# Attention values with the value rows stationary and two heads side by side in the array

## The reference, cut to what matters

```python
# A: 4 heads, two softmax maps each (8 maps), output o1 - lam * o2
# B: 6 heads, latent attention          C: 6 heads, masked by distance
sc = einsum('bhqd,bhkd->bhqk', q, k) * scale
p  = softmax(sc, axis=-1)
o  = einsum('bhqk,bhkd->bhqd', p, v)      # 512 queries, 512 keys, width 64
```

## Time and profile before

| | |
|---|---|
| runs | 3307.59, 3308.88, 3309.75 us; median 3308.88 us |
| span of the profiled execution | 3305.6 us |
| PE, PEld busy | 3211.9 us, 2951.7 us (97%, 89%) |
| DVE, ACT, POOL busy | 2540.6, 1302.2, 1956.7 us (77%, 39%, 59%) |
| attention of layer 0, first matmul to last wait | 139.49 to 310.69 us |
| attention of layer 1, the same | 1782.31 to 1954.07 us |

### The profile page before, as it was taken

How to read it: one execution, slowest core, us unless ns; L and a number is a source line. 1 busy time by engine, 2 the same in 40 slices (tenths; PEclk the granted TensorE clock), 3 DMA queues, 4 the chain that set the end, 5 groups by cost and what they waited for, 6 DMA issues and landing times. The chain is left out here.

```text
span 3305.6 us, 64644 instructions
## 1 busy us (share of the span) xinstructions
PE 3211.9 (97%) x18498; PEld 2951.7 (89%) x18502; DVE 2540.6 (77%) x5451; ACT 1302.2 (39%) x2060; POOL 1956.7 (59%) x1556
## 2 busy tenths in 40 slices
PE   8999999999999999999999999999999999999997
PEld 8898889999999888888798988899999998888886
DVE  1466567888888899999924656588888888999998
ACT  2355234444444433333323542344444443333333
POOL 3445338888654466666544453488886544666665
PEclk9999999999999999999999999999999999999999
DMA  4001138999787799999820021399997877999996
GB/s 166 30 1 77 39 89 293 324 324 320 242 299 249 258 337 338 335 335 335 280 102 26 1 77 52 100 319 318 322 315 249 290 253 253 340 338 337 337 333 226
DMA packets 249399, 765.14 MB, mean 231 GB/s; under 512 B 28384, under 2 KB 95712, under 8 KB 241376
## 3 DMA queue, kind: packets, MB, share of 16 engines
q1 hardware_dynamic: 170400, 459.95, 42.1%
q0 software_dynamic: 73728, 268.47, 21.6%
q10 hardware_dynamic: 5184, 35.65, 3.0%
HBM read 677.98 MB, written 85.98 MB: 231 GB/s over the span
## 5 line engine op out<-in xcount | busy, mean ns | idle before, releaser
L687 POOL TENSOR_TENSOR st_lo<-st_raw,st_hi 128x1024 fp32r<-128x1024 f32 x290 | 697.8, 2406 | 463.9 <-ACT st_hi L949 454.3
L949 ACT CAST st_hi<-st_raw 128x1024 fp32r<-128x1024 f32 x544 | 569.9, 1048 | 663.0 <-PE ps L1993 632.8
L1902 PE MATMUL ps<-t_hi,st_hi 128*128 128x384 f32 (+1 forms) x2288 | 794.7, 347 | 0.0
L1903 PE MATMUL ps<-t_lo,st_hi 128*128 128x384 f32 (+1 forms) x2288 | 786.0, 344 | 0.0
L795 POOL TENSOR_TENSOR wt_lo<-w_f,wt_hi 128x384 fp32r<-128x384 f32 x256 | 418.1, 1633 | 319.5 <-ACT wt_hi L1080 319.4
L1906 PE MATMUL ps<-t_hi,st_lo 128*128 128x384 f32 (+1 forms) x2288 | 462.7, 344 | 0.0
L1902 PEld LDWEIGHTS ps<-t_hi,st_hi 128*128 128x128 f32 x2288 | 430.1, 188 | 10.5
L1903 PEld LDWEIGHTS ps<-t_lo,st_hi 128*128 128x128 f32 x2288 | 430.1, 188 | 9.8
L1906 PEld LDWEIGHTS ps<-t_hi,st_lo 128*128 128x128 f32 x2288 | 408.5, 188 | 11.0
L992 ACT ACTIVATE h_out<-ps 128x384 f32<-128x384 f32 x256 | 125.7, 491 | 696.7 <-PE ps L1906 592.7
L1993 PE MATMUL ps<-st_hi,wt_hi 128*128 128x512 f32 x1536 | 390.8, 390 | 2.7 <-ACT wt_hi L1080 2.7
(11 more groups left out here) (219 smaller groups left out, 5104.8 us busy)
## 6 DMA issues: line engine op xcount, KB each, us to landing
st_raw<-in_peer_u SPq DMA_DIRECT2D x256, 512.0 KB
st_raw<-in_peer_v SPq DMA_DIRECT2D x256, 512.0 KB
gelu_d<-h_out SPq DMA_DIRECT2D x256, 192.0 KB
h_in<-gelu_d SPq DMA_DIRECT2D x256, 192.0 KB
gates_d<-g_stage ACTq DMA_DIRECT2D x32, 1024.0 KB
g_ch<-gates_d SPq DMA_DIRECT2D x56, 512.0 KB, 6.1
w_raw<-in_w_in SPq DMA_DIRECT2D x16, 1168.0 KB, 5.3
st_raw<-in_peer_w_q SPq DMA_DIRECT2D x32, 512.0 KB
```

Source lines behind the costliest of these rows:

```text
L687: nc.gpsimd.tensor_tensor(st_lo[:, s].rearrange("p c f -> p (c f)"), st_raw[:, r], st_hi[:, s].rearrange("p c f -> p (c f)").bitcast(F32), ...
L949: nc.scalar.copy(st_hi[:, r % 2].rearrange("p c f -> p (c f)"), st_raw[:, r]).then_inc(st_h, 1)
L1902: nc.tensor.matmul(dst, st_hi[:, s, c], t_hi[:, c, rows], start=c == 0, stop=False)
L1903: nc.tensor.matmul(dst, st_hi[:, s, c], t_lo[:, c, rows], start=False, stop=False)
```

## The change

`values` changes its roles: the 128x64 block of values is stationary and the 128x128 block of turned probabilities streams. The two jobs of a pair are taken together: the even job's output goes to PSUM partitions 0 to 63, the odd job's to 64 to 127, of bank 6 (128 x 512: two heads' width x queries). `p_t` therefore holds both jobs of a pair; it moves, with a new tile `o_t`, into the space of `t_hi` and `t_lo`, which is idle during the attention. When a pair is there, ACT copies the bank to `o_t` (`keep_ot`), PE turns it back with four 128x128 transposes into bank 7 (`turn_back`), and one DVE operation of 128x512 per pair scales it into `o_all` (`finish`), where there was one of 128x256 per job.

The order on PE changes with it. The four calls of `values` for pair i stand in the odd job of pair i (block 0) and in the even job of pair i+1 (blocks 1, 2 and 3); `turn_back(i-1)` stands in the odd job behind `turn_qk`. The loops over pairs on PE and DVE are written out. Core of the diff:

```diff
-            def values(i, s, qb, kind):
-                j = 2 * i + s
-                if qb == 0:
-                    pe.wait_ge(o_ev, JOBS * l + j + 1)
-                pe.wait_ge((pt_dve, pt_act)[qb % 2], 2 * (JOBS * l + j) + qb // 2 + 1 + 1)
+            def values(i, qb):
+                if qb == 0:
+                    pe.wait_ge(ot_ev, PAIRS * l + i)
+                pe.wait_ge((pt_dve, pt_act)[qb % 2], 2 * (JOBS * l + 2 * i + 1) + qb // 2 + 1 + 1)
                 for k in range(TB):
-                    last = nc.tensor.matmul(ps[:, 6 + s, qb * VD:(qb + 1) * VD], p_t[:, qb, k], v, start=k == 0, stop=k == TB - 1)
+                    for s in range(2):
+                        last = nc.tensor.matmul(ps[s * VD:(s + 1) * VD, 6, qb * P:(qb + 1) * P], value_of(i, s, k),
+                                                p_t[:, s, qb, k], start=k == 0, stop=k == TB - 1)
...
+            def turn_back(i):
+                pe.wait_ge(ot_ev, PAIRS * l + i + 1)
+                pe.wait_ge(o_ev, PAIRS * l + i)
+                for tb in range(TB):
+                    last = nc.tensor.transpose(ps[:, 7, tb * P:(tb + 1) * P], o_t[:, tb * P:(tb + 1) * P], ident[:])
+                last.then_inc(ob_ps, 1)
...
+            def even(i):
+                j, kind = 2 * i, kinds[i]
+                score(j, 0, 2, kind)
+                turn_p(j, 0)
+                if i > 0:
+                    values(i - 1, 1)
+                turn_qk(j + 1, 1, kind)
+                score(j, 0, 3, kind)
+                turn_p(j, 1)
+                if i > 0:
+                    values(i - 1, 2)
+                score(j + 1, 1, 0, kind)
+                turn_p(j, 2)
+                if i > 0:
+                    values(i - 1, 3)
+                score(j + 1, 1, 1, kind)
+                turn_p(j, 3)
+
+            def odd(i):
...
+                score(j, 1, 2, kind)
+                turn_p(j, 0)
+                if ahead is not None:
+                    turn_qk(j + 1, 0, ahead)
+                if i > 0:
+                    turn_back(i - 1)
+                score(j, 1, 3, kind)
+                turn_p(j, 1)
+                if ahead is not None:
+                    score(j + 1, 0, 0, ahead)
+                turn_p(j, 2)
+                values(i, 0)
+                if ahead is not None:
+                    score(j + 1, 0, 1, ahead)
+                turn_p(j, 3)
...
+            for qb in range(1, TB):
+                values(PAIRS - 1, qb)
+            turn_back(PAIRS - 1)
# ACT
+            def keep_ot(i):
+                act.wait_ge(pv_done, PAIRS * l + i + 1)
+                nc.scalar.copy(o_t[:], ps[:, 6]).then_inc(ot_ev, 1)
...
                 if ahead is not None:
                     exponent(j + 1, 1 - s, 0)
+                if last_pair is not None:
+                    keep_ot(last_pair)
+                if ahead is not None:
                     exponent(j + 1, 1 - s, 1)
...
+            keep_ot(PAIRS - 1)
             act.wait_ge(sub_ss, l + 1)
# DVE
-                nc.vector.tensor_tensor(o_all[:, :, ds(j * VD, VD)],
-                                        ps[:, 6 + s, 0:TB * VD].rearrange("p (t d) -> p t d", t=TB),
-                                        row_inv[:, s].unsqueeze(2).to_broadcast([P, TB, VD]),
-                                        ALU.mult).then_inc(o_ev, 1)
+                nc.vector.tensor_tensor(o_all[:, :, ds(2 * i * VD, 2 * VD)].rearrange("p t (s d) -> p t s d", s=2),
+                                        ps[:, 7].rearrange("p (t s d) -> p t s d", t=TB, s=2),
+                                        row_inv[:, turn].rearrange("p s t -> p t s").unsqueeze(3).to_broadcast(
+                                            [P, TB, 2, VD]), ALU.mult).then_inc(o_ev, 1)
```

More of the change, by code:

```diff
@@ L164, in build @@
     assert T_D * 2 * GCH == 2 * DC * T
+    p_t = nc.alloc_sbuf_tensor_at("p_t", [P, 2, TB, TB, P], F32, offset=keep.end - 2 * DC * T * 4)
+    o_t = nc.alloc_sbuf_tensor_at("o_t", [P, T], F32, offset=keep.end - 2 * DC * T * 4 + 2 * TB * T * 4)
+    assert (2 * TB + 1) * T <= 2 * DC * T
     ident = keep.tile("ident", [P, P], F32)
@@ L1251, in job @@
                 if before:
-                    invert_sums(j - 1, 1 - s)
+                    invert_sums(j - 1, 1 - s, turn if s else 1 - turn)
                 if ahead is not None:
                     score(j + 1, 0, ahead)
-                if before:
-                    finish(j - 1, 1 - s)
-                keep_pt(j, 2)
+                if last_pair is not None:
+                    finish(last_pair, 1 - turn)
+                keep_pt(j, s, 2)
                 if ahead is not None:
@@ L1263, in _, with pair @@
             score(0, 1, "A")
[L1264 to L1273, removed]
+            def pair(i, turn, kind, after):
+                first_pair = isinstance(i, int) and i == 0
+                job(2 * i, 0, kind, kind, turn, before=not first_pair)
+                job(2 * i + 1, 1, kind, after, turn, None if first_pair else i - 1)
+            pair(0, 0, "A", "A")
+            pair(1, 1, "A", "A")
+            pair(2, 0, "A", "A")
+            pair(3, 1, "A", "B")
+            pair(4, 0, "B", "B")
+            pair(5, 1, "B", "B")
+            pair(6, 0, "B", "C")
+            pair(7, 1, "C", "C")
+            pair(8, 0, "C", "C")
+            pair(9, 1, "C", None)
             dve.wait_ge(sub_q, l + 1)
             nc.vector.tensor_reduce(sub_sq[:], o_q.rearrange("p t h d -> p (t h) d"), AX_X, ALU.add).then_inc(sub_ss, 1)
-            invert_sums(JOBS - 1, 1)
-            finish(JOBS - 1, 1)
+            invert_sums(JOBS - 1, 1, 1)
+            finish(PAIRS - 1, 1)
             at = at + JOBS
@@ L1825, in values @@
                 if qb == TB - 1:
                     last.then_inc(pv_done, 1)
[L1828 to L1833, removed]
-                turn_p(j, 0)
-                if before is not None:
-                    values(last_i, 1 - s, 2, before)
+            def turn_back(i):
[4 more added lines that the diff above has]
+                last.then_inc(ob_ps, 1)
@@ L1837, in job @@
+            def odd(i):
+                j, kind = 2 * i + 1, kinds[i]
+                ahead = kinds[i + 1] if i + 1 < PAIRS else None
+                score(j, 1, 2, kind)
+                turn_p(j, 0)
                 if ahead is not None:
-                    turn_qk(j + 1, 1 - s, ahead)
-                score(j, s, 3, kind)
+                    turn_qk(j + 1, 0, ahead)
+                if i > 0:
+                    turn_back(i - 1)
+                score(j, 1, 3, kind)
                 turn_p(j, 1)
-                if before is not None:
-                    values(last_i, 1 - s, 3, before)
@@ L1854, in _ @@
             score(0, 0, 1, "A")
-            job(0, 0, "A", "A")
-            job(0, 1, "A", "A", "A")
-            before, first = "A", 1
-            for kind, after, end in (("A", "B", JA // 2), ("B", "C", (JA + JB) // 2), ("C", None, JOBS // 2)):
-                if before != kind:
-                    job(first, 0, kind, kind, before)
-                    job(first, 1, kind, kind, kind)
-                    first += 1
-                with pe.Fori(first, end - 1) as i:
-                    job(i, 0, kind, kind, kind)
-                    job(i, 1, kind, kind, kind)
-                job(end - 1, 0, kind, kind, kind)
-                job(end - 1, 1, kind, after, kind)
-                before, first = kind, end
-            values(JOBS // 2 - 1, 1, 2, "C")
-            values(JOBS // 2 - 1, 1, 3, "C")
+            for i in range(PAIRS):
+                even(i)
+                odd(i)
+            for qb in range(1, TB):
+                values(PAIRS - 1, qb)
+            turn_back(PAIRS - 1)
             pe.wait_ge(mix_ready, l + 1)
```

72 lines of the change are left out of this document (36 added, 36 removed).

## The result

The changed kernel takes 3282.1 us (median of four runs, 3281.2 to 3286.19), the kernel before 3308.84 us beside it: 26.7 us less, a ratio of 0.9923 with a 95% interval of 0.9911 to 0.9936. Forecast were 3295 us and a range of 3268 to 3345. The sign and the main mechanism held; the gain was about twice the one forecast.

The account below looks back on a forecast made before the run. PE was taken to bound the attention. Pairs were to save 18.9 us, less 1.1 us at layer borders and 3.6 us at layer ends: 14.2 us, from 3308.9 to 3295 us, range 3268 to 3345 us.

Parts of the forecast that it names:

- What bounds the kernel: In the attention, PE sets the pace of A and nearly that of B and C; DVE is the next limit.
- the point of no change: Length of a values burst on PE at which the change neither gains nor loses: 1.57 us.
- The stream: A burst's 16 matmuls on PE, both array halves working side by side: 0.96 us, or 1.71 us in a row.
- The switch: PE's change between full array and halves around each burst: 0.42 us per burst, ends 0 and 0.50.
- The pairs: Even plus odd attention job: 13.24 us in A, 17.76 in B, 16.26 in C, against 14.18, 18.55 and 17.38.
- The sum: Whole kernel: 18.9 us saved by pairs, less 1.1 and 3.6 us, gives 14.2 us and a 3295 us median.
- the borders of the layers: Each layer's first pair lacks three bursts, three stand at its end; 1.1 us taken off the gain.
- The end of the layers: After the last values, `keep_ot` delays ACT's table load and root: 1.8 us later per layer, 3.6 us in all.
- No cost: Moved `p_t`, written-out loops, waits on `ot_ev` and `o_ev`, and POOL's work were to add no time.
- The free switch: Rival: changing array shape on PE is nearly free, a burst costs 0.96 us; 3269 us, chance 0.13.
- Halves in a row: Rival: the array halves don't run side by side on PE; 3319 to 3352 us, middle 3335, chance 0.30.
- Overlap in part: Rival: loads and matmuls of both halves sometimes wait, bursts of 1.5 to 1.65 us; 3302 to 3315 us, chance 0.15.

Follow-up runs that it names:

- head by head: Changed kernel with each burst issuing all four key blocks of the even head, then all four of the odd head, instead of alternating: 3316.9 us.
- One half alone: Changed kernel without the odd head's matmuls in the values bursts, so its output isn't the attention: 3280.2 us.
- root first: Changed kernel with ACT's square root and its table load ahead of the last `keep_ot` of each layer: 3282.6 us.
- two bursts together: Changed kernel with two double bursts per pair instead of four single ones, blocks 0 and 1 in the odd job, 2 and 3 in the even: 3301.6 us.
- the split bursts: Changed kernel with each burst but a layer's last three cut in two, one part before and one behind the slot's four transposes: 3302.0 us.

## Why the prediction was right, and where it was off

**What bounds the kernel: right.** PE set the pace of the attention. Making its bursts dearer by 0.49 us cost 71 us per us (head by head), which is the forecast's slope of 73 and leaves the point of no change at 1.20 + 26.7 / 71 = 1.58 us, where the forecast had 1.57.

**The stream: right in kind, 0.10 us too dear.** The forecast kept the order of issue and took 0.214 us for a block of keys with one stream left over, 0.96 us. The halves start almost together, and eight pairs take 8 x 0.107 = 0.86 us. One half alone takes as long, which settles that they overlap.

**The switch: right in kind, 0.08 us too dear.** 0.17 us on either side, twice, is 0.34 us; what the forecast added on each side for part of a weight load doesn't show in the burst's 1.20 us. How the 0.34 us divide isn't shown further. The burst is then 0.86 + 0.34 = 1.20 us instead of 1.38. The burst is the term that was mis-sized: by the slope it is worth 0.18 x 73 = 13 us.

**The pairs.** A's even job was forecast at 7.74 us and takes 7.16 (168.36 to 175.52); with the measured burst the same working gives 7.20. Its odd job was forecast at 5.5 us, held by DVE, and takes 6.0. This step failed: not DVE but ACT held it. ACT has 2 us to spare per job, and that was taken as cover, while its order puts an exponent ahead of the queries that PE wants next; 0.5 us in 8 pairs, 4 us lost. Putting the queries first gave back 0.27 of the 0.5 us. That the pair of A came out at 13.16 us against the forecast 13.24 is luck: its even job was 0.6 us too dear and its odd job 0.5 us too cheap. B and C came out as worked: the idle times of the odd jobs were forecast at 0.8 and 1.1 us. These are the scores behind `turn_qk`, in an odd B job, an odd C job and an even C job, on PEld's timeline of the changed kernel:

```profile
226.75 0.19 PEld L1815 LDWEIGHTS ps<-k_a,q_a 96*128 96x128 f32 x1 [0.82 <-issue]
...
259.55 0.19 PEld L1811 LDWEIGHTS ps<-k_a,q_a 128*128 128x128 f32 x1 [1.15 <-ACT q_a L901]
...
267.99 0.19 PEld L1811 LDWEIGHTS ps<-k_a,q_a 128*128 128x128 f32 x1 [0.53 <-issue]
```

In C the row names ACT, but ACT's copy (from 257.98, 0.67 us) is over at 258.65. The last of DVE's three copies, on DVE's timeline, ends at 259.48, just before the score; it is DVE's chain, as forecast:

```profile
258.79 0.69 DVE L1216 CAST k_sw<-ps 64x512 fp32r<-64x512 f32 x1
```

With a burst of 1.20 us the forecast's own working gives pairs of 17.04 us in B and 15.7 in C, against 16.96 and 15.75. (A shorter burst covers less in C's even job: 2.48 - 0.9 - 1.20 = 0.4 us idle where 0.2 were counted. Measured is 0.53 us, of which 0.17 are the change of shape.)

**The sum.** Up to the last values the forecast had 18.9 - 1.1 = 17.8 us for both layers, measured were 2 x 14.1 = 28.2. The pairs give 8 x 1.02 + 6 x 1.59 + 6 x 1.63 = 27.5 us of it where the forecast had 18.9, and the borders of the layers 0.7 where it took off 1.1. So of the 10.4 us between, the borders, which the forecast had with the wrong sign, explain 1.8 (why they gain isn't shown). The shorter burst, taken through the forecast's own pairs (0.54, 0.72 and some 0.54 us less in A, B and C), explains 12, and the wait in A takes 4 back; what is left is half a us. The end of the layers was forecast at 3.6 us and cost 3.7. The size was right and the cause half right, so that the 1.85 us per layer agree with the forecast 1.8 is in part luck: the table load is one of two chains of nearly the same length (root first).

**No cost: right.** `keep_ot` is hidden in the even job, as argued; ACT's timeline of the changed kernel:

```profile
175.17 0.56 ACT L919 COPY o_t<-ps 128x512 f32<-128x512 f32 x1
176.34 0.72 ACT L909 ACTIVATE probs<-masked,neg_max 128x512 f32<-128x512 f32 x1 [0.61 <-DVE neg_max L1235]
```

The copy ends 0.6 us before the exponent behind it has its input from DVE.

**The rivals.** The free switch is out: 0.34 us of 1.20 are switch. Halves in a row are out by the 0.054 us between starts, and what they would have done is nearly what head by head shows, 3317 us, just under the forecast's 3319 to 3352. Overlap in part is what that order gives.

**The range.** 3268 to 3345 us holds a gain, no change and a loss, so that it held says little. The forecast's own range, 3283 to 3304 us for bursts of 1.2 to 1.5 us, was missed by 1 us: 3282 lies midway between the forecast's 3295 and the free switch's 3269.

## What to carry to other kernels

Two narrow products can share the array at no cost for the second, if their instructions alternate one by one; the price is the change of shape on either side, so put enough work between two changes. But where a burst stands in a software pipeline also decides which chain through the other engines it covers: three bursts behind `turn_qk`, where PE waited anyway, won 1.0 and 0.7 us per pair in B and C and lost 0.9 in A, and the bursts set two by two (two bursts together) lost in all three kinds. An engine with time to spare is no cover for a wait until its order has been read: ask what stands ahead of the one result that the busy engine needs next.

## What the runs showed of the hardware

A change between instructions that use all 128 columns and ones that use a half of 64 shows 0.17 us of idle weight loads each way, at full clock (once 0.24 in the split bursts); a second entry and exit cost 0.27 us net. Turning queries and keys (weights of 96 columns) after full-width work shows no such idle time in the rows above.

With eight instructions for one half ahead of eight for the other, the second half started early by only three (1.58 us against 1.09 alternated). The Trainium skill, TensorE: Matmul & The Clock Gate, The mechanism, says that matmuls start and end strictly in program order and that weight loads overlap with matmuls in flight only where the row groups differ. The first doesn't hold here from one half to the other: in head by head the odd head's first matmul starts at 177.392 us, ahead of three of the even head's that stand before it (177.496 to 177.714). The second doesn't as it stands: both halves here use the same 128 rows, and 16 weight loads and 16 matmuls share the same 0.86 us; the form that the same section has beside it, that loads are also pulled ahead into a background weight buffer, fits.
